# A gated FFN's down projection: seven half-size products in place of eight

## The reference

```python
def _conv_ffn(h, w_gu, conv_w, conv_b, w_down):
    g, u = jnp.split(h @ w_gu, 2, axis=-1)
    ...
    return (jax.nn.silu(gc) * u) @ w_down
...
    x = _affine_ln(ALPHA * x + gate2 * _conv_ffn(h, w_gu, conv_w, conv_b, w_down), ln2_g, ln2_b)
```

## Time and profile before

| | |
|---|---|
| Median of 3 runs | 2960.46 us (2954.57 to 2963.38) |
| The profiled execution's own time | 2957.74 us |
| its span, first to last instruction | 2955.9 us |
| what lies around the span | 1.8 us |
| TensorE busy, mean granted clock | 92% of the span, 0.963 |
| VectorE, ScalarE, POOL busy | 60%, 42%, 16% |
| ffn_down_phase | 2373.8 to 2955.9 us |

### The profile page before, as it was taken

One profiled execution on the slowest core, in us unless ns is written; L12 is line 12 of the kernel. 1 busy time (PEld: TensorE's weight loads), 2 busy tenths in 40 slices (PEclk: granted clock), 3 DMA queues, 4 the chain that ended last, 5 costly groups with the idle time before them and its releaser, 6 DMA issues. The chain is left out here.

```text
span 2955.9 us, 50052 instructions
## 1 busy us (share of the span) xinstructions
PE 2725.3 (92%) x17011; PEld 2475.6 (84%) x17011; DVE 1769.5 (60%) x3030; ACT 1232.2 (42%) x2612; POOL 471.0 (16%) x678
## 2 busy tenths in 40 slices
PE   4999999676999978996999999999999979999996
PEld 4999999565888866885999999999999968888875
DVE  4534332346999974777887876667666534352445
ACT  2211111115988971234555565556555522112121
POOL 0000000124444431223001000000000000230312
PEclk8999999887999998997999999999999989999999
DMA  8223222498675814563655564444444354334233
GB/s 290 82 92 120 79 92 64 169 358 176 137 153 118 162 50 149 185 197 86 226 176 170 166 205 151 151 153 149 151 151 155 107 173 139 107 128 139 85 126 130
DMA packets 400709, 435.71 MB, mean 147 GB/s; under 512 B 122592, under 2 KB 293654, under 8 KB 397848
## 3 DMA queue, kind: packets, MB, share of 16 engines
q1 hardware_dynamic: 377216, 414.28, 46.7%
q10 hardware_dynamic: 21016, 11.29, 1.3%
q0 software_dynamic: 2304, 7.88, 0.8%
HBM read 311.18 MB, written 124.57 MB: 147 GB/s over the span
## 5 line engine op out<-in xcount | busy, mean ns | idle before, releaser
L2202 PE MATMUL fu_alpha<-fu_h,fu_w 128*128 128x384 f32 x3168 | 576.3, 336 | 17.8 <-DVE fu_h L2428 10.6
L2688 PE MATMUL fd_acc<-fd_w,fd_f 128*128 128x512 f32 x2376 | 546.7, 392 | 28.5 <-DVE fd_w L2716 19.1
L2202 PEld LDWEIGHTS fu_alpha<-fu_h,fu_w 128*128 128x128 f32 x3168 | 555.1, 189 | 20.4 <-issue 20.3
L2688 PEld LDWEIGHTS fd_acc<-fd_w,fd_f 128*128 128x128 f32 x2376 | 447.4, 189 | 127.8 <-issue 19.1
L2202 PE MATMUL fu_beta<-fu_h,fu_w 128*128 128x384 f32 x1584 | 287.1, 335 | 0.6 <-DVE fu_h L2428 0.6
L2202 PEld LDWEIGHTS fu_beta<-fu_h,fu_w 128*128 128x128 f32 x1584 | 277.1, 189 | 1.1 <-issue 1.1
L598 PE MATMUL pj_gps<-pj_ht,w_in 128*128 128x256 f32 x2160 | 268.9, 285 | 0.0
L598 PEld LDWEIGHTS pj_gps<-pj_ht,w_in 128*128 128x128 f32 x2160 | 263.5, 191 | 1.3
L2712 DVE TENSOR_TENSOR fd_f<-fd_f_stage,fd_f 128x512 fp32r<-128x512 f32 (+1 forms) x110 | 91.5, 833 | 284.7 <-ACT fd_f L2668 284.7
L2668 ACT CAST fd_f<-fd_f_stage 128x512 fp32r<-128x512 f32 (+1 forms) x110 | 63.5, 579 | 443.5 <-PE fd_acc L2688 395.5
L2402 DVE TENSOR_TENSOR fu_w<-up_w_stage,fu_w 128x512 fp32r<-128x512 f32 x264 | 181.7, 689 | 85.6 <-ACT fu_w L2266 83.6
(11 more groups left out here) (221 smaller groups left out, 4125.6 us busy)
## 6 DMA issues: line engine op xcount, KB each, us to landing
up_w_stage<-in_w_gu_dram SPq DMA_DIRECT2D x88, 512.0 KB, 4.1
fu_w_sums<-w_gu_sums SPq DMA_DIRECT2D x132, 256.0 KB, 3.9
fd_w_stage<-in_w_down_dram SPq DMA_DIRECT2D x54, 512.0 KB, 3.7
fd_f_stage<-f_t SPq DMA_DIRECT2D x88, 256.0 KB, 2.6
at_k<-k_t SPq DMA_DIRECT2D x28, 704.0 KB, 13.0
w_gu_sums<-fu_w_sums SPq DMA_DIRECT2D x66, 256.0 KB, 4.8
fo_w<-in_w_ada_dram SPq DMA_DIRECT2D x8, 2048.0 KB, 18.1
up_w_stage<-in_w_gu_dram SPq DMA_DIRECT2D x44, 256.0 KB, 4.3
```

The source lines that it names most:

```text
L2202: mm = pe.matmul(out, w[x][:, j, k, :], b[y][:, j, k, :], start=opens and (k, x, y) == (0, HI, HI), stop=(k, x, y) == (KH - 1, LO, HI), sk ...
L2688: mm = pe.matmul(acc[:, t, at], f[a][:, slot, t * P:(t + 1) * P], w[b][:, w_at(st, slot), at], start=is_step(st, 0) and (a, b) == (HI, HI) ...
```

## The change

**In the up stage** f_t gets another layout, [token tile, channel, slice, token]. A store now writes pieces of one tile, 128 tokens to a channel. As a row of res begins one token ahead of a tile (the convolution's shift), one token of the tile ahead goes in a transfer of its own, and the last tile of a span is written with 127 tokens: two transfers in span 0, three in the others.

**In the down stage** the product f @ w_down is seen as 2x2 blocks: two token tiles (a pair, 9 in all) by two halves of 1408 channels (11 slices), times the two channel halves by two halves of 512 output columns. Seven products of block sums replace the eight block products. ORDER says in which order the seven forms go; each runs over all 9 pairs, so there are 63 units of 11 slices x 3 passes = 33 matmuls. A_OF and B_OF name the blocks that are added or subtracted ahead (f by VectorE, w_down by POOL). Each unit has a PSUM bank of its own, of eight in rotation. The result is gated into res, which holds all 18 tiles: form 5, 3 and 4 write their place of res straight from PSUM (BEGUN), the others go through tmp, and SUMS lists the additions. Form 3 adds ALPHA * x1 to the first tile of a pair, form 4 to the second (RESIDUAL), from a buffer of two halves scaled by ScalarE. Statistics are taken in forms 3, 7 and 6, and a tile is finished in form 7 (first of the pair) or 6 (second). ScalarE normalises, POOL multiplies and adds in place, SP stores from res. The last tile ends on VectorE. All loops are written out. w_down's first 11 slices are staged in the last tiles of res by ScalarE's queue, in three pieces; the first unit's f comes in three pieces too.

The diff, cut; the removed lines of ffn_down_phase are its whole body, shown above.

```diff
@@ ffn_up_phase, store, and the counts waited for
-                        sp.dma_start(f_t[rows, 0:SPAN - 1], res[:, par, 1:SPAN]).then_inc(stored[par], 16)
...
+                    per_span = SPAN // P
+                    t0, c0 = p * per_span, 1
+                    tiles = lambda n: f_t[t0:t0 + n, :, bass.ds(f, 1), :].rearrange("t p f c -> p t (f c)")
+                    of_tiles = lambda c, n: res[:, par, c:c + n * P].rearrange("p (t c) -> p t c", c=P)
+                    last = P - 1
+                    if p:
+                        with nc.allow_non_contiguous_dma(reason="one token of the tile ahead"):
+                            sp.dma_start(f_t[t0 - 1, :, bass.ds(f, 1), last:P].rearrange("p f c -> p (f c)"), res[:, par, 0:1]).then_inc(stored[par], 16)
+                    if p < SPANS - 1:
+                        sp.dma_start(tiles(per_span - 1), of_tiles(c0, per_span - 1)).then_inc(stored[par], 16)
+                        sp.dma_start(f_t[t0 + per_span - 1, :, bass.ds(f, 1), 0:last].rearrange("p f c -> p (f c)"),
+                                     res[:, par, c0 + (per_span - 1) * P:SPAN]).then_inc(stored[par], 16)
                     else:
-                        sp.dma_start(f_t[rows, t0:T_LAT], res[:, par, 0:LAT_TAIL + 1]).then_inc(stored[par], 16)
-                        sp.dma_start(f_t[rows, T_LAT:T_ALL], res[:, par, LAT_TAIL + 2:SPAN + 2]).then_inc(stored[par], 16)
+                        sp.dma_start(tiles(LAT_TAIL // P), of_tiles(c0, LAT_TAIL // P)).then_inc(stored[par], 16)
+                        t0 = T_LAT // P
+                        sp.dma_start(tiles(T_CTX // P), of_tiles(LAT_TAIL + 2, T_CTX // P)).then_inc(stored[par], 16)
...
-                        return (m - par) * 8 + 16
-                    return (m - par - p * FT) * 16 + (p * FT * 8 + 16)
+                    if p == 0:
+                        return (m - par) * 16 + 16
+                    return (m - par - FT) * 24 + (FT * 16 + 16)

@@ ffn_down_phase
+    ORDER = (5, 3, 1, 4, 7, 2, 6)
+    A_OF = {1: ((0, 0), (1, 1), ALU.add), 2: ((1, 0), (1, 1), ALU.add), 3: ((0, 0), None, None), 4: ((1, 1), None, None),
+            5: ((0, 0), (0, 1), ALU.add), 6: ((1, 0), (0, 0), ALU.subtract), 7: ((0, 1), (1, 1), ALU.subtract)}
+    B_OF = {1: ((0, 0), (1, 1), ALU.add), 2: ((0, 0), None, None), 3: ((0, 1), (1, 1), ALU.subtract),
+            4: ((1, 0), (0, 0), ALU.subtract), 5: ((1, 1), None, None), 6: ((0, 0), (0, 1), ALU.add), 7: ((1, 0), (1, 1), ALU.add)}
+    BEGUN = {5: ((0, 0, -1.0), (0, 1, 1.0)), 3: ((1, 1, 1.0),), 4: ((1, 0, 1.0),)}
+    SUMS = {5: (), 3: ((0, 1, ALU.add),), 1: ((0, 0, ALU.add), (1, 1, ALU.add)), 4: ((0, 0, ALU.add),), 7: ((0, 0, ALU.add),),
+            2: ((1, 0, ALU.add), (1, 1, ALU.subtract)), 6: ((1, 1, ALU.add),)}
+    RESIDUAL = {3: 0, 4: 1}
+    EARLY = {3: ((0, 1),), 7: ((0, 0),), 6: ((1, 0), (1, 1))}
+    TAILS = (7, 6)
+    UNITS = len(ORDER) * PAIRS
+    PIECES = ((0, 2), (2, 6), (6, KH))
+    AHEAD = 5
+    RING = KH + AHEAD
+    WSLOTS, XSLOTS, HSLOTS, BANKS = 3, 3, 2, 8
+    STAGED_AT = 12
...
+        f_lo = sb("fd_f_lo", [P, XSLOTS, KH, P], F32R)
+        f_hi = sb("fd_f_hi", [P, HSLOTS, KH, P], F32R)
+        f_more = sb("fd_f_more", [P, KH, P])
+        w = [sb(f"fd_w{h}", [P, RING, NH], F32R) for h in (HI, LO)]
+        wst = sb("fd_w_stage", [P, WSLOTS, 2, NH])
+        res = sb("fd_res", [P, 2 * PAIRS, D])
+        tmp = sb("fd_gated", [P, 2, NH])
+        xr = sb("fd_x1", [P, 2, NH])
...
+        def slices_first(u):
+
+            j, i = divmod(u, PAIRS)
+            return [j * KH + k for k in (KH - 2, KH - 1)] if i == 0 and 0 < j < len(ORDER) else []
+
+        def slices(u):
+
+            j, i = divmod(u, PAIRS)
+            if j >= len(ORDER) - 1:
+                return []
+            if i == PAIRS - 1:
+                return [(j + 1) * KH + k for k in range(AHEAD, KH - 2)]
+            return [(j + 1) * KH + i - 2] if 2 <= i < 2 + AHEAD else []
...
+        def w_slot_free(b):
+
+            j, k = divmod(b, KH)
+            return (j - 1) * (KH - AHEAD) + k - AHEAD + 1 if j and k >= AHEAD else None
...
+                def load_unit(u):
+                    if u >= XSLOTS:
+                        sp.wait_ge(unit_done, u - XSLOTS + 1)
+                    load_f(u)
+                    if sums_f(u) and u:
+                        sp.wait_ge(f_summed, sum_count(u) - 1)
+                        load_more(u, more_staged)
+
+                def load_w(b):
+                    s = (b - KH) % WSLOTS
+                    if b - KH >= WSLOTS:
+                        sp.wait_ge(w_low, b - WSLOTS + 1)
+                    first, second, _ = B_OF[ORDER[b // KH]]
+                    for at, block_of in enumerate((first, second)):
+                        if block_of is not None:
+                            kh, nh = block_of
+                            sp.dma_start(wst[:, s, at, :], w_blocks[kh, b % KH][:, half(nh)]).then_inc(w_staged[s], 16)
+
+                def load_x(u):
+                    t = 2 * pair(u) + RESIDUAL[form(u)]
+                    for nh in range(2):
+                        q = residual_count(u) + nh
+                        if q >= 2:
+                            sp.wait_ge(x_added, q - 1)
+                        sp.dma_start(xr[:, q % 2, :], x_tiles[t][:, half(nh)]).then_inc(x_staged[q % 2], 16)
...
+                for u in range(UNITS):
+                    if u + 2 < UNITS:
+                        load_unit(u + 2)
+                    if has_residual(u):
+                        load_x(u)
+                    for b in slices_first(u + 1) + slices(u + 1):
+                        load_w(b)
+                    if has_tail(u - 4):
+                        store(u - 4)
...
+                def high_f(u, piece=0):
+                    k0, k1 = pieces(u)[piece]
+                    if sums_f(u):
+                        act.wait_ge(f_summed, sum_count(u, piece))
+                    else:
+                        act.wait_ge(f_staged[u % XSLOTS], 16 * f_loads(u))
+                    if u >= HSLOTS:
+                        act.wait_ge(unit_done, u - HSLOTS + 1)
+                    act.copy(f_hi[:, u % HSLOTS, k0:k1, :], f_raw[:, u % XSLOTS, k0:k1, :]).then_inc(f_high, 1)
+
+                def high_w(b):
+                    if b < KH:
+                        act.wait_ge(w_first[[n for n, (k0, k1) in enumerate(PIECES) if k0 <= b < k1][0]], 16)
+                    elif sums_w(b):
+                        act.wait_ge(w_summed, w_sum_count(b))
+                    else:
+                        act.wait_ge(w_staged[(b - KH) % WSLOTS], 16 * w_loads(b))
+                    if w_slot_free(b) is not None:
+                        act.wait_ge(slice_done, w_slot_free(b))
+                    act.copy(w[HI][:, b % RING, :], w_source(b)).then_inc(w_high, 1)
+
+                def scale_x(u):
+                    for nh in range(2):
+                        q = residual_count(u) + nh
+                        act.wait_ge(x_staged[q % 2], 16 * (q // 2 + 1))
+                        act.activation(xr[:, q % 2, :], xr[:, q % 2, :], ACT.Copy, scale=ALPHA).then_inc(x_scaled, 1)
...
+                for u in range(UNITS):
+                    for b in slices_first(u):
+                        high_w(b)
+                    if u + 1 < UNITS:
+                        high_f(u + 1)
+                    for b in slices(u):
+                        high_w(b)
+                    if has_residual(u):
+                        scale_x(u)
+                    if has_tail(u - 2):
+                        normalise(u - 2)
+                normalise(UNITS - 2)
...
+                for u in range(UNITS):
+                    j, i = divmod(u, PAIRS)
+                    if u >= BANKS:
+                        pe.wait_ge(gated, u - BANKS + 1)
+                    for k in range(KH):
+                        begins = [n for n, (k0, _) in enumerate(pieces(u)) if k0 == k]
+                        if begins:
+                            pe.wait_ge(f_low, f_count(u, begins[0]))
+                        if i == 0:
+                            pe.wait_ge(w_low, j * KH + k + 1)
+                        at = (j * KH + k) % RING
+                        for a, b in PASSES:
+                            stationary = f_hi[:, u % HSLOTS, k, :] if a == HI else f_lo[:, u % XSLOTS, k, :]
+                            mm = pe.matmul(acc[:, u % BANKS, :], stationary, w[b][:, at, :], start=(k, a, b) == (0, HI, HI),
+                                           stop=(k, a, b) == (KH - 1, LO, HI))
+                        if i == PAIRS - 1 and k < KH - AHEAD:
+                            mm.then_inc(slice_done, 1)
+                    mm.then_inc(unit_done, 1)
...
+                def low_f(u, piece=0):
+                    k0, k1 = pieces(u)[piece]
+                    dve.wait_ge(f_high, f_count(u, piece))
+                    dve.tensor_tensor(f_lo[:, u % XSLOTS, k0:k1, :], f_raw[:, u % XSLOTS, k0:k1, :],
```

(95 more changed lines are left out.)

326 lines of the change are left out of this document (141 added, 185 removed).

## The result

The changed kernel takes **3018.23 us** (median of 4 runs, 3016.78 to 3022.78) against 2961.92 for the kernel before on the same chip: ratio 1.0200, 95% interval 1.0188 to 1.0212. It is slower, as the likelier side of the prediction said, but by 56 us and not by 13, and it lies above the range of 2930 to 3005. The profiled execution took 3016.79, span 3015.0.

A forecast was written before the change was run, and what follows sets the result against it. The stage was taken as TensorE-bound. Unit 1's start plus 62 units gave 2862.1 us; waits and changes made 2954.1, the end and up stage 2969.1 of span, median 2974; range 2952 to 3000, with rivals 1 and 4 2930 to 3005.

The forecast's parts named there:

- TensorE's part: Down stage: 2079 matmuls, 297 fewer, at 0.2278 us; 7.52 us a unit, 63 units 473.5 us.
- the term for the changes of form: Down stage, between forms: late weight slices hold up the next unit; six changes cost 24 us (12 to 36).
- x1 loop: Forms 3 and 4: two x1 halves reloaded, scaled and added each unit make units 9.0 us, 21 us in all.
- The meetings with POOL: Forms 7 and 6: POOL and VectorE exclude each other; units of 10.6 and 10.9 us cost 25 and 20 us.
- rival 1: Forms 7 and 6: VectorE keeps POOL out, units 8.0 us, 45 becomes about 9, giving 2938; chance 0.25.
- The tail: After the last matmul: gate, add, statistics, normalising with POOL's last affine locked between, and store take 14 us (12 to 17).
- Start: Down stage's beginning: unit 1 starts near 2396 us, bounds 2393 and 2400, after first loads, sums and casts.
- The up stage: Stores of f in 512-byte and four-byte pieces cost 1 us at the end, bounds 0 and 10.
- Rival 2: Down stage: TensorE stays the bound, lock, loop and changes all hide, 92 becomes some 17: 2899 us; chance 0.05.
- Rival 3: Forms 7 and 6: gaps lower TensorE's clock; staying at 1.2 GHz adds 62 us, giving 3036; chance 0.06.
- Rival 4: DMA at 325 to 330 GB/s leaves no slack; changes of form and up stage reach upper ends: 2996; chance 0.14.

The follow-up runs named there:

- x1 last: Changed kernel with SP issuing slices 9 and 10 ahead of the x1 loads in each form's last unit: 3014.31 us, ratio 1.0190.
- slices early: Changed kernel with slices 9 and 10 ahead of next f on SP, slices 5 to 7 ahead of cast and gate: 2993.61 us, ratio 1.0115.

## Why the prediction was right and wrong

**TensorE's part was right.** A unit takes 7.48 us (7.52), the matmuls are 2079, and no unit is bound by anything else in forms 5, 1 and 2 away from their changes.

**The step that failed is the term for the changes of form**: "Five such and one unsummed change: 24 us (12 to 36)" measured 85.8. The mechanism was named (slot, queue, landing, three engines, then gate and low_f); its size was missed, in every change. In us from the start of the last unit (2453.0 and 2540.5):

| step | predicted | out of form 5 | out of form 3 |
|---|---|---|---|
| load of slice 8 issued | 5.4 | 5.0 | 12.5 |
| slice 10 landed | 12.8 | 15.8 | 28.2 |
| low_f through, TensorE goes on | 18.1 | 21.3 | 33.1 |

The walk was right up to slice 8 where no x1 loop came before, and it is 3 us short from there to the landing: 8.6 lost for 3.0. Behind the x1 loop its very first line was wrong.

Four things were left out. First, the loads of slices 5 to 7: I let these be copied by 6.7, as if they were there, but on SP they stand behind an x1 load that waits for the loop. They landed 7.9 to 10.9 us into the unit and were copied by 2555.5, 15.0 from the start, with 4.09 us for the three beside POOL's sums. Secondly, the order of the queue: x1's load waits ahead of slices 9 and 10 too, and I had listed only the f bytes there; by "x1 last" this alone counts for little. Thirdly, "at the 388 GB/s that the trace reached": this was a rate of a stretch with little else to do. From 2555 to 2569 the transfers ran at 294 GB/s with the DMA engines 0.85 busy; the transfer of slice 10 took 6.71 us and the median of its kind 5.2, twice the 2.6 of the earlier trace rows. Fourthly, the clock behind the gaps, 12 us of the 85.8 at most. Behind the first two stood the assumption that engines arrive at a change of form with their full lead; out of forms 3 and 4 the x1 loop had eaten it. What made the change out of form 2 (15.4) dearer than those out of forms 5 and 1 was not separated. The experiments bear that out: keeping the slices gives 88 us back, halving their bytes 20, no POOL sum 30, four x1 places 8 beyond the loop itself, no affine some 12 beyond its own units and the end (43 less the 22 and 9 that they lost), 7 of it in units 47 and 48. How these parts share each single change was not separated.

**The x1 loop was right**: 21 predicted, 24 measured, units of 8.7 to 12.0 us; with four places it is gone.

**The meetings with POOL: right in kind and period, too large in number.** I walked 10.6 and 10.9; the trace has 10.3 and 10.4. But five units of form 7 and four of form 6 lost 22 us for the 45 predicted. POOL's first multiplications of the two forms fall in units 39 and 56, the fourth and third unit of the form, which the count of 8 for form 7 had left out, and the first stretched units (8.6 and 9.9 us) lost less than the period says. The last two affines of form 7 fall in units 46 and 47: the 6.9 us of units 47 and 48, which went with the affine, belong to this term, 29 in all, and leave 79 for the changes. The timeline of the changed kernel in the last form, POOL and VectorE alone:

```profile
2962.28 2.39 POOL L2960 TENSOR_TENSOR fd_res<-fd_res,fd_ln_g 128x1024 f32<-128x1024 f32 x1
...
2963.07 3.08 DVE L2843 TENSOR_TENSOR fd_f_lo<-fd_f_raw,fd_f_hi 128x1408 fp32r<-128x1408 f32 x1 [0.84 <-ACT fd_f_hi L2754]
...
2964.75 3.63 POOL L2962 TENSOR_TENSOR fd_res<-fd_res,fd_ln_b 128x1024 f32<-128x1024 f32 x1
2966.07 2.85 DVE L2874 TENSOR_TENSOR fd_res<-fd_res,fd_gated 128x512 f32<-128x512 f32 x1
...
2968.96 1.29 DVE L2892 BATCH_NORM_STATS2 fd_stats<-fd_res 128x6 f32<-128x512 f32 x2
```

low_f begins while POOL multiplies and ends 1.5 after it; POOL's addition, 2.39 by itself, gets in behind low_f and takes 3.63; the addition of 0.68 takes 2.85. Each waits out the other's whole instruction, then has its turn; statistics (0.70 at most) and gates from PSUM (0.69 at most) never stretch. That settles rival 1: VectorE does not keep POOL out. Of the Trainium skill's section (SBUF — State Buffer, "Who interferes with whom") the mutual exclusion agrees with these rows; of its order of issue the rows show alternation only.

**The tail**: 18.5 for 14. POOL stood a unit behind, in the affine of the last tile but two, when the last statistics were ready, and its rstd for the last tile came at 3004.5. I had counted one affine there, two stood.

**The small terms.** Start 2397.8 for 2396. The up stage 0 for 1: 461,380 packets in place of 400,709 in the whole program, with no time lost. Rival 2 is excluded. Rival 3 as I put it (clock down through forms 7 and 6) did not come: both have 0.92 and 0.89; but the gaps at the changes brought the clock down to 0.50 behind them (0.73 is the mean of the 24 us shown), which is the upper bound of 24 us above, for 3.5 in the kernel before. I had priced this only for forms 7 and 6. Rival 4 (2996) had the right place, changes of form at their upper end, yet bytes alone account for 20 us of it, and the up stage did not slip. Two sums of the prediction are slightly off and change nothing: its high ends add up to 3032, not 3028, and the terms of the x1 loop to 8.46.

## What to carry to other kernels

At a change of phase, walk each in-order queue from the state in which the phase before leaves it, not from an engine with its full lead: buffers of depth one, waits of neighbours in the queue and the load under which a transfer runs add up there. A load that was placed early enough in the program can still be late because another one stands ahead of it and waits; and moving work to the front of an engine's order helps only if its data are there, as units 17 and 35 of "slices early" show. What costs nothing inside a phase (a sum on POOL, a second block) has its full price where a phase's first tiles are on the path. If two engines shut each other out, as POOL and VectorE do here, count their meetings in the critical unit and move the work to the engine that does it in fewer or shorter instructions.

## What the hardware showed that was not expected

- A 256 KB load took 5.2 us in the median and 6.7 at the change of form, for 2.6 before; right behind 2 x 704 KB ("x1 last") up to 9.3. The mean of the stretch, 213 GB/s and 0.60 of the DMA engines, hides that they stood idle at 2551 to 2553 (0.00) and ran at 0.85 and 294 GB/s from 2555 to 2569: what is ahead in the queue has to be moved first.
- After a gap of 10.63 us two matmuls that take 0.61 took 1.22: the granted clock is 0.50, the lower level of 1.2 GHz, from 2561 to 2573 us, and 1.00 again from 2575. Many short gaps cost twice in this way: 24 us of slow matmuls in the stage for 3.5 before.
- The stores of the up stage in rows of 512 bytes, with a column of 4-byte pieces in 44 steps, cost nothing that the trace shows: the up stage's matmuls span 977.4 us (977.5 before), and the down stage begins within 0.6 us of where it did.
